# The chunks' triangular inverse: each level takes only the 32 of 64 columns that it changes

## What is computed

```python
def rwkv7_step(state, inp):
    r_t, w_t, k_t, v_t, kk_t, ka_t = inp
    sa = jnp.einsum('bhvk,bhk->bhv', state, -kk_t)
    state = (state * w_t[:, :, None, :] + sa[..., None] * ka_t[:, :, None, :]
             + v_t[..., None] * k_t[:, :, None, :])
    return state, jnp.einsum('bhvk,bhk->bhv', state, r_t)
```

## Time and profile before

| | |
|---|---|
| median of 3 runs | 1594.3 us (1593.42 to 1595.28) |
| the profiled execution: time, span | 1593.52 us, 1591.8 us |
| TensorE products busy | 1542.9 us, 97% of the span, 16258 records |
| VectorE, ScalarE, GpSimd busy | 860.8 us, 686.1 us, 118.4 us |
| granted TensorE clock | 0.997 over the span |

### The profile page before, as it was taken

The page is one execution under the profiler, slowest core; times in us unless marked ns, Lnnn a source line. Parts: engine busy times, 40 slices in busy tenths (PEclk is TensorE's granted clock), DMA queues, the critical chain, the costliest instruction groups (busy, mean ns, idle before and its releaser), DMA issues.

```text
span 1591.8 us, 38944 instructions
## 1 busy us (share of the span) xinstructions
PE 1542.9 (97%) x16258; PEld 1451.2 (91%) x16258; DVE 860.8 (54%) x1471; ACT 686.1 (43%) x1103; POOL 118.4 (7%) x257
## 2 busy tenths in 40 slices
PE   8999999999999999999999999999899999999998
PEld 7999889899699999999999899975599999999886
DVE  5579744443556666666233334356646666666222
ACT  5565233333545444444222466456635444443111
POOL 1450392300000000000000000000000000000000
PEclk9999999999999999999999999999999999999999
DMA  5222000000123323333332122240023333333331
GB/s 153 67 67 80 22 4 4 4 4 4 44 80 93 91 82 91 92 92 90 101 91 78 54 79 79 80 137 2 1 71 100 87 89 89 92 92 107 101 91 71
DMA packets 210748, 113.65 MB, mean 71 GB/s; under 512 B 8032, under 2 KB 207410, under 8 KB 210642
## 3 DMA queue, kind: packets, MB, share of 16 engines
q1 hardware_dynamic: 210034, 109.93, 23.9%
q10 hardware_dynamic: 608, 2.16, 0.4%
HBM read 109.95 MB, written 2.13 MB: 70 GB/s over the span
## 4 chain that ended last, share of the span: by engine, by line
PE 89%; ACT 5%; DVE 3%; issue 2%; SPq 1%; DMA 0%; ACTq 0%; DVEq 0%
PE BK L664 87%; PE BK L1181 2%; ACT XB L1239 1%; ACT PTT L1239 1%; ACT L1239 1%; SPq L394 0%; ACT WHI L1239 0%; DVE MQA L1736 0%; DVE U L2202 0%; DVE WLO L1736 0%; ACT ALL L1239 0%; PE BK L1120 0%; ACT PR L1239 0%; DMA PRAW<-in_ffn_conv_b_dram 0%; DVE XB L1736 0%
## 5 line engine op out<-in xcount | busy, mean ns | idle before, releaser
L1736 DVE TENSOR_TENSOR WLO<-RAW,WHI 128x1024 fp32r<-128x1024 f32 (+1 forms) x182 | 236.3, 1298 | 163.5 <-ACT WHI L1239 162.5
L1239 ACT ACTIVATE WHI<-RAW 128x1024 fp32r<-128x1024 f32 (+1 forms) x182 | 202.5, 1112 | 210.6 <-PE BK L664 210.4
L664 PE MATMUL BK<-YNH,WHI 128*128 128x264 f32 (+1 forms) x1216 | 252.0, 288 | 1.3 <-DVE CUM L1740 1.3
L664 PE MATMUL BK<-YNL,WHI 128*128 128x264 f32 (+1 forms) x1216 | 248.1, 285 | 0.0
L664 PE MATMUL BK<-YNH,WLO 128*128 128x264 f32 (+1 forms) x1216 | 247.9, 285 | 0.0
L664 PE MATMUL BK<-XNH,WHI 128*128 128x258 f32 (+1 forms) x1056 | 216.3, 286 | 2.6 <-DVE PB L1736 2.0
L664 PE MATMUL BK<-XNH,WLO 128*128 128x258 f32 (+1 forms) x1056 | 213.4, 284 | 0.0
L664 PE MATMUL BK<-XNL,WHI 128*128 128x258 f32 (+1 forms) x1056 | 212.8, 283 | 0.0
L664 PEld LDWEIGHTS BK<-YNH,WHI 128*128 128x128 f32 x1216 | 190.9, 189 | 3.1 <-DVE CUM L1740 1.6
L664 PEld LDWEIGHTS BK<-YNL,WHI 128*128 128x128 f32 x1216 | 189.1, 189 | 0.0
L664 PEld LDWEIGHTS BK<-YNH,WLO 128*128 128x128 f32 x1216 | 188.9, 189 | 0.0
(11 more groups left out here) (292 smaller groups left out, 2192.0 us busy)
## 6 DMA issues: line engine op xcount, KB each, us to landing
RAW<-in_ffn_w_up_dram SPq DMA_DIRECT2D x88, 512.0 KB, 3.9
RAW<-in_ffn_w_down_dram SPq DMA_DIRECT2D x32, 704.0 KB, 4.8
RAW<-in_odd_w_in_dram SPq DMA_DIRECT2D x24, 512.0 KB, 3.9
RAW<-in_even_w_in_dram SPq DMA_DIRECT2D x22, 512.0 KB, 3.9
CB<-cum_dram SPq DMA_DIRECT2D x8, 528.0 KB, 8.2
RAW<-in_even_w_out_dram SPq DMA_DIRECT2D x8, 512.0 KB, 4.0
RAW<-in_odd_w_out_dram SPq DMA_DIRECT2D x8, 512.0 KB, 4.1
XIN<-in_x_dram ACTq DMA_DIRECT2D x4, 512.0 KB, 5.1
```

What stands on the lines that cost most here:

```text
L664: return pe.matmul(o, l, r, start=start, stop=stop, skip_group_check=check)
L1239: return nc.scalar.activation(o, i, f, **kw)
L1736: return nc.vector.tensor_tensor(o, x, y, op)
```

## The change

Of the 64 columns of the inverse a level changes only those of the first halves of its block pairs, and of the transpose only those of the second halves: 32 columns each. The changed kernel takes only these:

- two views: `part(ap, n, r)` gives the columns of the halves r, runs of b = 2 << n columns with gaps of b; `halved` gives 32 adjacent columns for each pair of heads in PSUM in the same shape;
- `residue` and `corrected` on TensorE stream 32 columns instead of 64 (read with the gaps) and write 32 adjacent columns. What is loaded as weights stays 64x64;
- VectorE's mask takes 96 columns for a group instead of 192;
- ScalarE's one copy of 384 columns becomes two copies of 96, one for the inverse and one for the transpose; at a chunk's last level one of 96 takes the place of one of 192;
- TM gets one matrix for each level ([LEVELS, PAIRS, C]) and another place in memory. Its columns of the second halves are constant and are set once by GpSimd with 30 small operations, behind the clearing of SS0; TensorE waits for those of level n before the first correction of that level in chunk 0 (`tm_init`).

```diff
+        def halved(b, lo, n):
+
+            return BK[:, b, HC * lo:HC * (lo + G3)].rearrange("p (m q c) -> p m q c", m=G3, c=2 << n)
+
+        def part(ap, n, r):
+
+            b = 2 << n
+            if len(ap.shape) == 2:
+                return ap.rearrange("p (q r c) -> p q r c", r=2, c=b)[:, :, r, :]
+            return ap.rearrange("p m (q r c) -> p m q r c", r=2, c=b)[:, :, :, r, :]
...
+                for n in range(LEVELS):
+                    for m in range(PAIRS):
+                        x = po.tensor_scalar(part(TM[:, n, m, :], n, 1), part(ID64[:, :], n, 1), -1.0, None, ALU.mult)
+                    x.then_inc(S("tm_init"), 1)
...
                         for h in HEADS:
-                            x = mm(BK[h, 2 + 2 * g, C * q:C * q + C], AT[h, c % 2, p, :], XB[h, c % 2, g, 0, q, :])
+                            x = mm(BK[h, 2 + 2 * g, HC * q:HC * q + HC], AT[h, c % 2, p, :],
+                                   part(XB[h, c % 2, g, 0, q, :], n, 0))
...
                     pe.wait_ge(S(f"t_mask{g}"), LEVELS * c + n + 1)
+                    if c == 0 and g == 0:
+                        pe.wait_ge(S("tm_init"), n + 1)
...
-                                mm(BK[h, 3 + 2 * g, C * q:C * q + C], XB[h, c % 2, g, 1, q, :], TM[h, p, :])
+                                mm(BK[h, 3 + 2 * g, HC * q:HC * q + HC], XB[h, c % 2, g, 1, q, :],
+                                   part(TM[h, n, p, :], n, 0))
...
-                            x = mm(BK[h, 3 + 2 * g, C * (G3 + q):C * (G3 + q) + C], TM[h, p, :], XB[h, c % 2, g, 1, q, :])
+                            x = mm(BK[h, 3 + 2 * g, HC * (G3 + q):HC * (G3 + q) + HC], TM[h, n, p, :],
+                                   part(XB[h, c % 2, g, 1, q, :], n, 1))
...
-                    if last:
-                        fn(XB[:, c % 2, g, 1, :, :], cols(3 + 2 * g, G3), ACT.Copy, scale=-1.0).then_inc(S(f"x_up{g}"), 1)
-                    else:
-                        fn(XB[:, c % 2, g].rearrange("p a q t -> p (a q t)"), BK[:, 3 + 2 * g, 0:2 * G3 * C], ACT.Copy,
-                           scale=-1.0).then_inc(S(f"x_up{g}"), 1)
+                    for a in range(1 if last else 0, 2):
+                        x = fn(part(XB[:, c % 2, g, a, :, :], n, a), halved(3 + 2 * g, G3 * a, n), ACT.Copy, scale=-1.0)
+                    x.then_inc(S(f"x_up{g}"), 1)
...
-                    tt(TM[:, G3 * g:G3 * g + G3, :], cols(2 + 2 * g, 0), over(LVL[:, n, :]), ALU.mult)\
-                        .then_inc(S(f"t_mask{g}"), 1)
+                    mask = part(LVL[:, n, :], n, 0)
+                    b = list(mask.shape)
+                    tt(part(TM[:, n, G3 * g:G3 * g + G3, :], n, 0), halved(2 + 2 * g, 0, n),
+                       mask.unsqueeze(1).to_broadcast([P, G3, b[1], b[2]]), ALU.mult).then_inc(S(f"t_mask{g}"), 1)
```

More of the change, by code:

```diff
@@ L42 @@
 LEVELS = 5
+HC = C // 2
 S5_L = 4
@@ L221, in decoder_trunk @@
         BKV = z("BKV", 2, PAIRS, 3, C)
-        TM = z("TM", PAIRS, C)
         SA = z("SA", PAIRS, C)
@@ L232, in decoder_trunk @@
         KT1 = z("KT1", S5_L, P)
+        TM = z("TM", LEVELS, PAIRS, C)
         assert z.pos[0] <= zpos
```

## The result

| | before | after |
|---|---|---|
| median (lowest to highest), 8 runs each | 1594.09 us (1592.84 to 1595.34) | 1599.93 us (1593.64 to 1601.42) |
| after / before | | 1.0032 (95% interval 1.0021 to 1.0044) |
| the profiled execution: time, span | 1593.52, 1591.8 us | 1601.42, 1599.6 us |
| granted TensorE clock over the span | 0.997 | 0.988 |

The forecast was 1590.3 us, the range 1586.0 to 1594.5. The time lies above it, beside rival (e), which had 3%.

A forecast was written before the change was run, and what follows sets the result against it. TensorE, holding 89% of the last-ending chain, was taken to bound the kernel, its steps paced by weight loads. Copies and tail (3.9 us) plus mask (0.1) gave 4.0 us off 1594.3: 1590.3 us, range 1586.0 to 1594.5.

The forecast's parts named there:

- rival (e): Chunk stage, after the scans: half the streaming columns drop TensorE's clock to 1.2 GHz for one chunk, 10 us lost, 1600; 3%.
- The steps: TensorE's pairs of head records: the 64-column weight load still paces them, 0 ns gained a step; other end 4.0 us.
- The tail: End of a product group: 32-column products drain sooner (192 ns, not 218), so ScalarE's copy starts 26 ns earlier per level.
- ScalarE's pair of copies: Copy into XB: two overlapping copies of 96 columns take about 400 ns instead of 490, 90 ns less on 34 levels.
- The mask: VectorE: 96 columns take 258 ns instead of 357, hidden nearly everywhere; 0.1 us gained once, behind the scans.
- The wait: TensorE waiting for ScalarE's copy into XB: to fall from 0.28 to some 0.17 us each.
- The stride: Reads and writes with holes: nothing, since two values share each 16 bytes; at worst 1.5 us plus 1.8 us at level 0.
- GpSimd's 30 operations: Setting TM's constant columns ahead of CPW: at most 10.1 us, CPW at most 1.9 us later, no cost.
- The sum: 34 levels x (90 + 26) ns = 3.9 us, plus 0.1 us of mask: 4.0 us gained, 1590.3 us.
- rival (d): TensorE's stream and ScalarE's writes: holes cost as in UIN at every level, copy pair about 594 ns, 1603.2 us; 7%.
- The step that failed: TensorE's granted clock in the chunk stage: expected to stay 0.98 from 190 to 400 us, so nothing in the total.
- The comparison by records: Chunk stage: 66 product records in 3.4 us at the low clock against 94 for the whole stage, pricing a low-clock chunk at 10 us.

The follow-up runs named there:

- run 5: Kernel before plus eight blocks of extra products, varying columns loaded and streamed: 58.3 ns a step for (64,64) and (64,32), 31.7 for (32,32).
- run 1: Changed kernel, but TensorE streams and writes all 64 columns again; copies and masks pick their 96 columns out of PSUM: 1589.04 us, ratio 0.9965.
- run 3: Changed kernel, but every 32-column view takes adjacent columns without holes (computes another matrix, same work): 1595.17 us, ratio 1.0002.
- run 2: Changed kernel with chunk 0 alone in the old form (64 columns in products, copies and masks): 1589.18 us, ratio 0.9964.
- run 4: Kernel before with the new form in chunk 0 alone, GpSimd's 30 operations included: 1599.11 us, ratio 1.0021.

## Why the prediction was wrong, point by point

**The steps** (0 gain, other end 4.0 us): right but for one step in a level, which the next point takes up. The groups stand 0.35 us apart as before, and run 5 isolates the cause.

**The tail** (26 ns a level): right in size, but by luck, since the mechanism is another. After's chunk is 0.10 us shorter than that of run 1, 25 ns for each of four levels, and the two differ only in what streams. The copy does not start earlier behind its products, though. In run 1 the last group of g1's correction starts at 344.62 and the copy 0.56 us later; in after, in the timeline above, these are 344.98 and 345.54, again 0.56 us. By single records the last one lasts 218 ns in run 1 and 219 in after, where 192 was forecast, and the copy starts 265 and 266 ns behind its start. The first group of the correction is where the time is saved: to the start of the next it is 0.35 us in run 1 (343.57 to 343.92) and 0.32 in after (343.95 to 344.27). Run 1:

```profile
343.57 0.52 PE L681 MATMUL BK<-TM,XB 64*64 64x64 f32 x12
...
343.92 0.52 PE L681 MATMUL BK<-XB,TM 64*64 64x64 f32 x12
...
344.62 0.52 PE L681 MATMUL BK<-XB,TM 64*64 64x64 f32 x12
...
345.18 0.39 ACT L1259 ACTIVATE XB<-BK 128x96 f32<-128x96 f32 x2 [0.27 <-PE BK L681]
```

In that group of after the first pair of head records starts at 343.952 us and the second 31 ns later; only from there on are the steps 58 ns. The loads come every 58 ns throughout. In run 1 each product starts 56 ns behind its load; in after this holds for the first pair, and from the second on it is 29 ns. So where half columns follow full ones, half a step is saved once, in each correction, and the load paces the rest. The forecast took the lengths of records for the time of draining. Run 5 says what they follow: with 64 columns loaded they last 220 ns for 64 and for 32 columns streamed, with 32 and 32 193 ns.

**ScalarE's pair of copies** (400 ns): right. In after 154 copies average 251 ns and the pair spans 0.40 us. Run 1, which has the copies and the masks but not the half columns, takes 0.40 us from a chunk, four times 0.10, where 0.09 was forecast. The groups of ScalarE and VectorE that answer and the earlier trace rows, and the wait that answers the earlier trace rows:

```profile
L1261 ACT ACTIVATE XB<-BK 128x96 f32<-128x96 f32 x154 | 30.2, 251 | 25.8 <-PE BK L681 25.7
```

```profile
L1756 DVE TENSOR_TENSOR TM<-BK,LVL 128x96 f32<-128x96 f32 x86 | 22.0, 257 | 71.5 <-PE BK L681 70.7
```

```profile
PEld BK L681 <- ACT XB L1261: 9.0, 38, 0.5
```

The mask was forecast at 258 ns and took 257. The wait fell less than forecast, from 0.28 to 9.0/38 = 0.24 us instead of 0.17; the low stretches are in it. What of it belongs to them was not taken apart.

**The stride** (nothing): right, by runs 3 and 5. The Trainium skill's rule of 16-byte lines (Advanced Engine Details and Errata, section Memory Cachelines), that two hits on a line are free, now has its row for the case of two: 31.6 ns against 31.7.

**GpSimd's 30 operations** (at most 10.1 us, at no cost): right, 7.49 us, and the powers CPW start at 186.21 instead of 186.08 us:

```profile
177.92 7.49 POOL L607 TENSOR_SCALAR TM<-ID 128x32 f32<-128x32 f32 x30
186.21 0.62 POOL L616 TENSOR_TENSOR CPW<-CPW,LAM 128x256 f32<-128x256 f32 x1 [0.80 <-DVE CPW L1756]
```

**The sum**: forecast 4 x 0.116 = 0.46 us a chunk, measured 22.94 - 22.45 = 0.49. The parts of the balance in which the change gains add up to 3.7 us, where 3.9 was forecast; the 0.1 us of the mask behind the scans can't be told apart there. Of the two terms the copies are right by their mechanism, the tail only by its size. (In rival (d) a pair 198 ns above 400 would be 598 ns, not 594; nothing hangs on it.)

**The step that failed** is the clock, put at nothing in the sum ("clock 0.98 from 190 to 400 us") and left to rival (e) with 3%. The runs showed 0.93 there: 6.4 us lost in chunk 0, 3.3 behind the scans (+2.76 against the -0.50 of other chunks) and 1.7 behind the stage, against the 3.7 gained. The mechanism of (e) and even its rough size were written down (a chunk at the low clock, 10 us, 1600). Two readings of it do not bear the weight:

- The one argument against it was "from 411.80 to 427.50 the slow UIN reads leave the array half empty and the clock holds 1.00". Of those 171 records only 40 read UIN, at 128x128 and 132 columns; 128 read U and CPW, at 128x32, and 3 are others. They say nothing of 64x64 products whose columns are halved. The rows that would have borne on it are the stage's own.
- The comparison by records, 66 in 3.4 us at the low clock against 94 in the stage as a whole, took the stage for one thing. It isn't. Of the kernel before, in chunk 0 (194.04 to 212.00), the three largest groups are the halved ones:

```profile
L664 PE MATMUL BK<-XB,AT 64*64 64x64 f32 x120 | 5.6, 225 | 0.6
L664 PE MATMUL BK<-XB,TM 64*64 64x64 f32 x120 | 5.0, 218 | 0.0
L664 PE MATMUL BK<-TM,XB 64*64 64x64 f32 x96 | 4.2, 219 | 0.0
```

They are 336 of the 508 records there, two thirds. In a later chunk of before (334.05 to 356.99 us) the same 336 have company (`solved`, `stepped`: SA, BKV, SS and others) and are 336 of 680, a half. So the change takes the largest share of columns exactly where TensorE has little else, and the first thing to weigh was chunk 0 by itself. These rows could not say whether the clock would fall, but nothing in them supported a chance as low as 3%. The range, too, stopped at 1594.5, short of a mechanism that had been written down with its price.

Rival (e) named one chunk, after the scans. What came is chunk 0, the stretch behind the scans at double its length, and the piece behind the stage. The price by records holds where the records are the stretch's own: 17.1 us with 302 records in place of 488 are 17.1 x (1 - 302/488) = 6.5 us of work lost, and 6.4 were measured. The piece behind the stage is a low stretch of 3.4 us at 441.4 us and whatever else differs there; it was not followed further.

**What stays open.** That in chunk 0 the clock falls with the half columns and holds with the full ones, at an unchanged pace of instructions, is shown (after against runs 1 and 2; run 4 against before). Half columns mean fewer values read and fewer written to PSUM; no run tells these apart. Which measure of activity the chip uses, and why the fall comes in most executions but not in all, is open as well.

## What to carry to other kernels

Where TensorE is paced by its weight loads, streaming fewer columns buys next to nothing in the step (here 27 ns a level), and can cost the clock. Before taking columns away, go through the kernel stage by stage and look for stretches in which the shortened products are most of TensorE's work; leave the full form there (in chunk 0 it costs 0.1 us, or 0.5 with the old copies), and take the narrow form where other products fill in. Whether the same holds where TensorE has just stood still is open: of the three traces with half columns behind the scans two have the longer low stretch, and one does not. When a rival is argued away, the rows against it must be of the same kind of product in the same place.

## What was not expected of the hardware

- The granted clock went to 0.50 for 17.1 us in a stretch in which two thirds of the products are 64x64 fp32 ones with 32 columns each; with 64 columns at the same step of 58.3 ns it stayed at 1.00. The Trainium skill (TensorE: Matmul & The Clock Gate, section The HAM clock gate) lays the low clock to an idle TensorE; the stretch of chunk 0 has no such pause ahead of it that before doesn't have as well. From 192.00 to 195.60 us TensorE is busy 2.12 us in after and 2.15 in before.
- At 1.2 GHz the load-paced step is 107 ns (0.64 us for 6), with 32 columns streamed as with 64: the groups of after in chunk 0 stand as far apart as those of before behind its scans, so the weight loads slow down by the same share as the products. Before:

```profile
289.72 0.85 PE L664 MATMUL BK<-TM,XB 64*64 64x64 f32 x12
290.36 0.85 PE L664 MATMUL BK<-XB,TM 64*64 64x64 f32 x12
```

- The same program has the fall in some executions and not in others, so single runs scatter by up to 0.8% (run 4: 1592.95 to 1606.24 us), each at its own clock. Here the clock beside a time says more than the time.
- VectorE's operation XB<-AT,M1T, with both operands in SBUF, takes 1.25 us where an operation of GpSimd's rotation of U runs beside it to its end, and 0.36 us in most other chunks. In before and after this happens on the way from chunk 1 to chunk 2, where the interval is long (24.4 and 24.1 us); in run 1, whose chunk 1 begins elsewhere against GpSimd's work, it doesn't, and the interval is 22.77 us. That the one makes the other is read from the times alone. The timeline of after, first VectorE, then GpSimd:

```profile
235.86 1.25 DVE L1756 TENSOR_TENSOR XB<-AT,M1T 128x192 f32<-128x192 f32 x1
```

```profile
235.57 1.32 POOL L662 TENSOR_TENSOR FT<-U,FC 128x528 f32<-128x528 f32 x1
```
